# Where TensorE loads the registers for the next item's expert and form in a mixture-of-experts loop

## The reference

```python
def expert_block(args):
    xblk, e = args
    gate = xblk @ w_gate[e] + b_gate[e]
    up = xblk @ w_up[e] + b_up[e]
    gate = jnp.minimum(gate, SWIGLU_LIMIT)
    up = jnp.clip(up, -SWIGLU_LIMIT, SWIGLU_LIMIT)
    h = (up + 1.0) * gate * jax.nn.sigmoid(SWIGLU_ALPHA * gate)
    return h @ w_down[e] + b_down[e]

yb = lax.map(expert_block, (xb, block_e)).reshape(P, D)
y = jax.ops.segment_sum(yb.astype(jnp.float32) * row_w[:, None], row_tok, num_segments=T + 1)[:T]
```

## Time and profile before

| | us |
|---|---|
| median of 3 runs | 2549.87 |
| lowest and highest run | 2547.91, 2552.31 |
| profiled execution, own time | 2550.04 |
| its span, first to last instruction | 2548.0 |
| TensorE busy in the span | 2373.1 (93%) |
| VectorE, ScalarE, GpSimd busy | 718.8, 497.8, 421.9 |
| mean granted TensorE clock, as a share of 2.4 GHz | 0.965 |

### The profile page before, as it was taken

How to read it: one execution, slowest core, us unless ns; L and a number is a source line. 1 busy time by engine, 2 the same in 40 slices (tenths; PEclk the granted TensorE clock), 3 DMA queues, 4 the chain that set the end, 5 groups by cost and what they waited for, 6 DMA issues and landing times.

```text
span 2548.0 us, 31938 instructions
## 1 busy us (share of the span) xinstructions
PE 2373.1 (93%) x11116; PEld 1208.7 (47%) x11140; DVE 718.8 (28%) x1230; ACT 497.8 (20%) x1116; POOL 421.9 (17%) x529
## 2 busy tenths in 40 slices
PE   5999999998987699999999999999999999999992
PEld 3575756774553344444444444344444444444430
DVE  4155565372465120111121111111111211111114
ACT  5122213223442110111111111111111111111112
POOL 5000000003004711111121121121111111111112
PEclk9999999999986799999999999999999999999996
DMA  8112110136023676677789989889988998999985
GB/s 281 33 34 75 34 53 22 58 100 235 34 115 112 240 254 215 213 255 255 259 293 375 333 296 371 307 312 354 335 275 277 315 330 302 371 327 340 323 315 201
DMA packets 216274, 587.80 MB, mean 231 GB/s; under 512 B 21339, under 2 KB 81267, under 8 KB 216211
## 3 DMA queue, kind: packets, MB, share of 16 engines
q1 hardware_dynamic: 131650, 337.94, 36.0%
q10 hardware_dynamic: 55504, 197.22, 20.6%
q0 software_dynamic: 29056, 51.75, 9.5%
HBM read 548.46 MB, written 38.37 MB: 230 GB/s over the span
## 4 chain that ended last, share of the span: by engine, by line
PE 87%; DVE 4%; DMA 2%; issue 2%; ACT 2%; another core or an unknown queue 1%; POOL 1%; ACTq 0%; SPq 0%; DVEq 0%; POOLq 0%
PE ps L1896 25%; PE ps L1923 13%; PE ps L1955 12%; PE ps L1969 7%; PE ps L1652 5%; PE ps L1753 4%; PE ps L1648 4%; PE ps L1658 2%; PE ps L1709 2%; PE ps L1655 2%; PE ps L1934 2%; PE ps L1859 2%; DMA w_up_e<-in_w_up_dram 1%; PE ps L1891 1%
## 5 line engine op out<-in xcount | busy, mean ns | idle before, releaser
L1896 PE MATMUL ps<-w_gate_e,xT 128*128 128x512 f32 x736 | 346.3, 593 | 0.0
L1896 PE MATMUL ps<-w_up_e,xT 128*128 128x512 f32 x736 | 345.8, 592 | 0.0
L1955 PE MATMUL ps<-w_down_e,hT 128*128 128x512 f32 x736 | 319.7, 592 | 0.0
L1473 DVE TENSOR_SCALAR oh_gu<-part_e,tab_e 128x128 bf16<-128x128 f32 x48 | 13.7, 286 | 1001.4 <-PE ps L1896 627.5
L1028 ACT ACTIVATE sig_sb<-gate_sb 128x1024 f32<-128x1024 f32 x47 | 49.7, 1057 | 1066.9 <-DVE gate_sb L1479 1066.8
L1923 PE MATMUL ps<-w_gate_e,xT 128*32 128x256 f32 (+1 forms) x1504 | 229.9, 475 | 4.0 <-DMA w_up_e<-in_w_up_dram 3.8
L1923 PE MATMUL ps<-w_up_e,xT 128*32 128x256 f32 (+1 forms) x1504 | 227.9, 471 | 0.8 <-issue 0.8
L1896 PEld LDWEIGHTS ps<-w_up_e,xT 128*128 128x128 f32 x736 | 139.8, 190 | 176.0 <-issue 176.0
L1896 PEld LDWEIGHTS ps<-w_gate_e,xT 128*128 128x128 f32 x736 | 140.2, 190 | 168.8 <-issue 165.6
L1955 PEld LDWEIGHTS ps<-w_down_e,hT 128*128 128x128 f32 x736 | 138.0, 190 | 165.0 <-issue 165.0
L1969 PE MATMUL ps<-w_down_e,hT 128*32 128x256 f32 (+1 forms) x1504 | 191.1, 475 | 5.7 <-issue 5.7
(11 more groups left out here) (384 smaller groups left out, 2354.5 us busy)
## 6 DMA issues: line engine op xcount, KB each, us to landing
w_down_e<-in_w_down_dram ACTq DMA_DIRECT2D x368, 512.0 KB, 4.6
w_gate_e<-in_w_gate_dram SPq DMA_DIRECT2D x256, 512.0 KB
w_up_e<-in_w_up_dram SPq DMA_DIRECT2D x256, 512.0 KB
w_ring<-in_w_ada_dram SPq DMA_DIRECT2D x17, 1024.0 KB, 5.2
w_ring<-in_w_in_dram SPq DMA_DIRECT2D x20, 512.0 KB, 5.4
w_first<-in_w_ada_dram SPq DMA_DIRECT2D x7, 1024.0 KB, 12.3
x_all<-in_x_dram SPq DMA_DIRECT2D x2, 2048.0 KB, 10.7
w_out<-in_w_out_dram SPq DMA_DIRECT2D x8, 512.0 KB, 8.7
```

The lines of the kernel that those rows point to most:

```text
L1896: last = T.matmul(ps[:, b, :], xT[:, k, :], wgt[b // 2][:, k, (b % 2) * 512:(b % 2) * 512 + 512], start=False, stop=k == KT - 1)
L1955: last = T.matmul(ps[:, 4 + b, :], hT[:, k, :], wgt[2][:, k, b * 512:b * 512 + 512], start=k == 0, stop=k == KT - 1)
```

## The change

In the loop, the line that loads `e` and `v` of item i+2 moves from behind `down(i, v_down)` to the head of the iteration, ahead of the load of `v_down`. The three register loads then stand together ahead of `rows(i + 2)`. Nothing else is changed; the tail is as it was.

```diff
             with pe.Fori(0, n_before) as i:
+                e, v = item_expert(pe, i + 2), item_variant(pe, i + 2)
                 v_down = item_variant(pe, i)
                 rows(i + 2)
                 down(i, v_down)
-                e, v = item_expert(pe, i + 2), item_variant(pe, i + 2)
                 gate_up(i + 2, e, v)
```

## The result

The changed kernel takes 2557.94 us (median of 6 runs, 2554.88 to 2562.34), the kernel before 2549.23 us (6 runs, 2544.86 to 2552.31). The ratio is 1.0037, with a 95% interval of 1.0026 to 1.0049: slower by 8.7 us. The profiled execution took 2560.32 us against 2550.04, so 10.3 us more. The forecast was 2553.6 us in a range up to 2557.5, and "no change" as the likeliest class; it was wrong.

What follows compares the result with a forecast made beforehand. The loop was taken to be bound by TensorE's matmuls and the gaps between them. Losses of 6.8 and 3.2 us less 6.35 saved gave +3.65 us, so 2553.6 us forecast, range 2547.5 to 2557.5.

Steps and rivals of the forecast that it cites:

- The bound: Whole loop: it lasts as long as TensorE's matmuls and gaps; TensorE busy 1560.27 of 1580 us.
- The places: Hidden behind both saves 6.35 us; rows behind both loses 6.8, behind quarter 3.2; whole, half and first iteration 0.
- The price of a load: At the moved loads: 0.42 us each, 0.85 for the two, with 0.64 and 1.3 as ends.
- The rule for a pair of p us: Whole loop: the sum is about 7p - 2.3 up to p = 0.97 and 8p - 3.3 above.
- the sum's terms: Over the loop: 6.8 us lost behind both, 3.2 behind quarter, 6.35 saved ahead of hidden, together +3.65.
- Comparison (a): Rows behind both: gap 0.12 us in the tail without a load, 0.44 with one; a load is at least 0.32.
- Comparison (b): Behind both: hidden with two loads has gap 0.83 us, rows with one 0.44; difference 0.39, one load less head instructions.
- (c): Loop's head, bound from above: if the branch back costs 0.26 us more, a load is 0.39 + 0.26 = 0.65.
- The second, a dear load: Rows behind both and quarter: a load of 0.6 us or more is paid in full, 2556.2 to 2557.0 us; chance 0.21.
- The first, overlap of loads that stand together: Loop's head: second and third load cost less than the first, -1.3 us, 2548.6; chance 0.14, with a nearly free load.
- The third, cover at the starts: Rows behind both: a wait for xg or hT hides the pair, only the saving stays, -6.35 us, 2543.5; chance 0.09.

Runs made afterwards that it cites:

- the third run: The kernel before with the load of v_down moved from the loop's head to between rows and down: 2533.64 us, ratio 0.9993.
- the first run: The kernel before with only the load of e moved to the head, v still loaded behind down: 2537.82 us against 2536.24, ratio 1.0004.

## Why the prediction was wrong

- **The bound.** Right: the loop lasts as long as TensorE's matmuls and the gaps between them. The 10.3 us more of the profiled execution are 18.1 us of added gaps less 7.7 us of gaps that went.
- **The places.** Right: 8 starts behind both and 4 behind quarter pay, 8 hidden behind both gain, starts behind whole and half don't grow (only the run with one load moved has one behind half, after waits for weights), the 4 waits for xT stay, and the first iteration moves by little (second down at 903.29 us in place of 902.16, which takes in its own 1.6 us of idle ahead of rows).
- **The price of a load. This is the step that failed.** I took 0.42 us, 0.85 for the two, with 1.3 as the upper end. One load with its checks costs 0.75 us, the pair 1.5. The rule for a pair of p us, 8p - 3.3 above p = 0.97, gives +8.7 us at p = 1.5, which is the measured difference by luck: above p = 1.2 it is wrong, because the savings with both next also end, at the 1.2 us that these gaps have to give. With that the sum at p = 1.5 is 12 x 1.5 - 0.2 lost and 3 x 0.70 + 1.0 + 3 x 1.21 + 1.47 = 8.2 saved, +9.6 us, and the traces show +9.8 at these places and +10.3 in all. With p put right, the sum's terms hold.
- **Comparison (a)**, the tail without a load against the head with one, gave 0.32 and was called a lower end. It was one: 0.43 us more were hidden, as the third run shows. To take a lower end for the neighbourhood of the value was the mistake: the quarter starts, with no idle time at all beside one load, had said that the sequencer is at the edge there, and rows at an edge say nothing of how much lies on the hidden side.
- **Comparison (b)**, two loads behind down against one at the head, gave 0.39, and **(c)** added 0.26 for the loop's branch back. (c) was called a bound from above, 0.65 for a load, and so 1.3 for the pair and 2557.5 for the range: it was none, since a load costs 0.75. With a load at 0.75 the head must have about 0.36 us of other work that the place behind down lacks (0.75 - 0.39), if the cover is alike at both. This is worked out, not shown: no run took the head's own instructions away. By these figures it was chance that (a) and (b) came out alike, and I had counted it as evidence.
- **The range checks.** The compiled order ahead of the prediction shows two instructions behind each load. They are a third of the price, and I let them pass as part of a load whose size I then took from differences. Without them a load is 0.47.
- **The rivals.** The second, a dear load, is what happened, at the place and by the mechanism that it named, beyond the price that it was given (0.6 to 0.65). The first, overlap of loads that stand together, falls by the first run: the second moved load costs as much as the first. The third, cover at the starts, falls by the changed kernel's rows.
- **The pages.** The Trainium skill (Runtime: NRT & Kernel Launch, Instruction fetch mechanics) has about 200 ns for a register load; the runs show 0.47 us for one from SBUF with its address and without checks. The Trainium skill (DMA: Bandwidth & Descriptors, Latency and other measured facts) has a floor of about 600 ns for a tensor_load; the 0.47 us lie below it, and with checks a load measures 0.75, and 0.64 to 0.69 where the address is at hand. (At 0.4 us for the pair the prediction's own terms give +1.4 us, not +1.1.)

## What to carry to other kernels

A register load is sequencer work of much the same size wherever it stands (0.64 to 0.77 us here), and what it costs depends on what the array has left to do at that place: put it behind long matmuls, never just ahead of a loop's or a branch's end behind short ones, and carry values in registers instead of loading them again. Where a place is at the edge of its cover, taking an instruction away and adding one have different prices; a difference between two rows then bounds the price only from below, and it takes an added instruction to measure it. Moving work to where gaps are already open can't gain unless the place that it leaves has more of them.

## What the runs showed of the hardware

- TensorE's sequencer took 0.64 to 0.77 us for a value load with its two range checks, 0.13 to 0.14 us for a check, 0.25 to 0.27 us for a branch that is passed. Loads that stand together did not overlap (0.75 and 0.77 us).
- It led the array by some 15 to 19 matmuls of the trace with their weight loads, so that cover goes by the matmuls that are queued and is not one time: 3.1 us more behind 64-column matmuls than behind 32-column ones, and 3.3 more again behind 128-column ones.
- After gaps of 2.2 to 2.5 us TensorE came back at 1.2 GHz in 3 of 8 places (eight transposes in 1.91 us instead of 1.06), while after one of 2.74 us it did not; after gaps of 4.4 to 8.5 us in the run with ten more loads it was at 1.2 GHz in most places (1.94 us). The gaps ahead of rows of up to 1.8 us in the changed kernel left the clock at 2.4 GHz. No one length of gap parts the two: in the run with ten more loads the clock fell shortly after two gaps of 1.7 and 2.0 us too.
